# Partition sums in the second modulation: products with a column of ones instead of transposes and a VectorE sum

## The chip, the cores and the metric

The kernel runs on one core of a Trainium2 chip. The metric is the device time of one execution in microseconds; several executions are timed and the median is taken. One execution is recorded by the hardware profiler. The engines are TensorE (PE, with its weight loads listed apart as PEld), VectorE (DVE), ScalarE (ACT), GpSimd (POOL) and SyncE (SP).

## The reference

One layer of a hybrid backbone for 256 latent tokens and 256 context tokens of width 2048, all in float32. What matters here is the conditioning. A vector `c` of 2048 elements gives six modulation vectors of 2048 elements each:

```python
def adaln(cond, w_mod, b_mod):
    m = (jax.nn.silu(cond) @ w_mod + b_mod).reshape(cond.shape[:-1] + (6, D_MODEL))
    return tuple(jnp.expand_dims(m[..., i, :], -2) for i in range(6))

sh1, sc1, gt1, sh2, sc2, gt2 = adaln(c, w_mod[l], b_mod[l])
hx = modulate(rms_norm(x, g_mix[l]), sh1, sc1)
# ... four token mixers on hx @ w_in, gates, sum, output projection ...
x_mixed = x + gt1 * merge_branches(...)
hx2 = modulate(rms_norm(x_mixed, g_ffn[l]), sh2, sc2)
x = x_mixed + gt2 * swiglu(hx2, w_ffn_gate[l], w_ffn_up[l], w_ffn_down[l])
```

`sh1` and `sc1` are needed at once and are made at the start of the kernel. `gt1`, `sh2`, `sc2` and `gt2` are needed much later; making them is the "second modulation".

## The kernel before

**Weights as pieces.** All large weight matrices come in pieces of 128 x 1024 float32 (512 KB) through a ring of four slots. SP loads a piece into `RAW`. ACT rounds it to `HI` (L438), DVE subtracts to get `LO` (L771), and PE multiplies: each exact float32 product is made of three products of rounded operands, the three lines L1344 to L1346 and L1372 to L1374. Semaphore `lo_done` releases PE and also SP's next load; `used`, given by PE, lets ACT overwrite the slot.

**Stages.** First modulation and input products with it (to about 150 us), input projections with attention, pooling and LRU steps between the pieces (to about 440 us), a mixing loop `pe.Fori(1, 4)` whose first pass is unrolled ahead of it (to about 820 us), the output projection (to about 907 us), then the gated feed-forward part. Every engine has its order written out by hand: DVE and PE run through the same piece numbers `w`, and small steps are called after given pieces.

**Second modulation.** A group `g` is 512 columns of `w_mod`. POOL loads it in 16 row tiles of 128 x 512 (L408). DVE multiplies each tile by its 128 elements of silu(c), one per partition, and adds it to an accumulator (`mod_tile`, L871 and L873), so that after 16 tiles the 512 wanted numbers are the sums of the accumulator's columns over its 128 partitions. Groups 0 to 11 (`gt1`, `sh2`, `sc2`) are finished by two helpers; the last four (`gt2`) take another way and are not touched.

- `mod_turn(g, acc, bank)` on PE (L1490 to L1495) waits until the 16 tiles are in, transposes the four 128 x 128 blocks of the accumulator into one bank of PSUM (`turn`, L1340: the block is the loaded weight, the identity is streamed), and signals `mod_turned`.
- `mod_columns(g, bank)` on DVE (L876 to L882) waits for that, sums the 128 x 4 x 128 numbers over the innermost axis (L880), waits for its own result, adds the bias (L882) and signals `mod_read`. The results are four columns of `MC2`.

**Where they stand.** Group 0: PE after piece 44, DVE after piece 47 of the input projections (about 290 us). Groups 1 to 9: three per pass of the mixing loop, on PE after pieces 2, 17 and 28 (`MOD_TURN_AT`), on DVE after 6, 21 and 32 (`MOD_READ_AT`). Groups 10 and 11: in the output projection, on PE after pieces 12 and 27, on DVE after 17 and 31. `a2()` (L1112) needs group 11, and the feed-forward part's first step needs `a2`.

**Other small products that the prediction uses.** `mod1_turn` (L1439) multiplies a 128 x 128 float32 block, as weight, by 4 streamed columns (`PICK`); it belongs to the first modulation. `h2_turn` (L1725) multiplies 128 x 128 float32 blocks of tokens by a diagonal matrix of 128 columns. `mod_unit` (L1426) streams 256 columns against weights of 32 columns. L930 and L931 are the mask and the row maximum of the attention scores.

`Own` counts a DVE semaphore for waits of the engine on its own results; `own.enter` and `own.leave` only do arithmetic on that count for a loop.

Of the kernel before, what the change touches and what calls it, by code (L numbers as in the profile page):

```python
# [25 lines left out]
ALU = mybir.AluOpType  # L26
ACT = mybir.ActivationFunctionType
AX_X = mybir.AxisListType.X

P = 128  # L30
# [100 lines left out]
def build(nc, x, c, ctx, c_ctx, w_mod, b_mod, g_mix, g_ffn, g_final, w_in, w_pool, pool_scale,  # L131
# [3 lines left out]
    with ctxs:  # L135
        def sb(name, shape, dt=F32):
            return ctxs.enter_context(nc.sbuf_tensor(name, shape, dt))

        def sem(name):
            return ctxs.enter_context(nc.semaphore(name))  # L140
# [13 lines left out]
        PA = sb("PA", [P, P])  # L154
# [3 lines left out]
        MC2 = sb("MC2", [P, 4 * KT])  # L158
        A2 = sb("A2", [P, KT])
        EPSC = sb("EPSC", [P, 1])  # L160
        ST = sb("ST", [P, 64])
# [61 lines left out]
        ps = ctxs.enter_context(nc.psum_tensor("ps", [P, 8, BW], F32))  # L223
# [30 lines left out]
        def s(name):  # L254
            if name not in S:
                S[name] = sem(name)
            return S[name]
# [507 lines left out]
        def _(dve):  # L765
            own = Own(dve, own_v)
            tt, ts, stt = dve.tensor_tensor, dve.tensor_scalar, dve.scalar_tensor_tensor

            def low(p, j):
                dve.wait_ge(hi_done, p + 1)  # L770
                tt(LO[:, j % RING, :], RAW[:, j % RING, :], HI[:, j % RING, :], ALU.subtract).then_inc(lo_done, 1)  # L771
# [7 lines left out]
            dve.memset(ST[:, 48:49], 0.0).then_inc(lo_done, 1)  # L779
            dve.memset(ST[:, 49:50], 0.0).then_inc(lo_done, 1)  # L780
            dve.memset(RP, 0.0).then_inc(s("rp_zero"), 1)
            own.did(dve.memset(SCP, 0.0))
            own.did(dve.memset(SHP, 0.0)); own.wait()
            dve.wait_ge(s("cst_in"), 16)
# [76 lines left out]
            def mod_tile(g, k, acc):  # L861

                if isinstance(g, int) and g < EARLY:
                    src = MR[:, k % 2, :]
                    dve.wait_ge(s(f"mod_landed{k % 2}"), g * (KT // 2 * 16) + 16 * (k // 2 + 1))
                else:
                    src = MR4[:, k % 4, :]
                    dve.wait_ge(s(f"mod4_landed{k % 4}"), g * (KT // 4 * 16) + 16 * (k // 4 + 1 - EARLY * KT // 4))
                if k:
                    dve.wait_ge(s("mod_used"), g * KT + (k + 2))  # L870
                    i = stt(acc, src, SCF[:, 0, k:k + 1], acc, ALU.mult, ALU.add)  # L871
                else:
                    i = ts(acc, src, SCF[:, 0, k:k + 1], None, ALU.mult)  # L873
                i.then_inc(s("mod_used"), 1)

            def mod_columns(g, bank):  # L876

                dve.wait_ge(s("mod_turned"), g + 1)
                sums = MC2[:, bass.ds(g * 4, 4)]
                own.did(dve.reduce_sum(sums, ps[:, bank, :].rearrange("p (k n) -> p k n", k=4), AX_X))  # L880
                own.wait()
                tt(sums, sums, PA[:, bass.ds(g * 4 + 32, 4)], ALU.add).then_inc(s("mod_read"), 1)  # L882

            def straight(w):
                if w == 18:
# [16 lines left out]
                if w == 47:  # L902
                    mod_columns(0, 0)
# [154 lines left out]
            def merge(f, n, b):  # L1058

                dve.wait_ge(used, f * BLK + (MIX0 + 34 + 2 * n + 4))  # L1060
                dve.wait_ge(s("gate_read"), f * 4 + (n + 1))
                m = flat(MG[:, 3, :])
                if n == 0:
                    if not isinstance(f, int):
                        dve.wait_ge(s("mg_turned"), f)
                    tt(m, pair(b), flat(S4[:, n, :]), ALU.mult).then_inc(s("merge_read"), 1)
                    dve.wait_ge(s("merge_read"), f * 4 + (n + 1))
                    dve.memset(ST[:, 54:55], 0.0).then_inc(s("merge_add"), 1)
                else:
                    tt(flat(S4[:, n, :]), pair(b), flat(S4[:, n, :]), ALU.mult).then_inc(s("merge_read"), 1)  # L1070
                    dve.wait_ge(s("merge_read"), f * 4 + (n + 1))
                    dve.wait_ge(s("merge_add"), f * 4 + n)
                    tt(m, m, flat(S4[:, n, :]), ALU.add).then_inc(s("merge_add"), 1)
# [11 lines left out]
            dve.memset(ONES, 1.0).then_inc(s("branches_made"), 1)  # L1085

            with dve.Fori(1, 4) as f:
                own.enter(f, 1, 3)
                for w in range(BLK):
                    low(f * BLK + (MIX0 + w), w % 4)  # L1090
                    for t in MOD_AT[w]:
                        mod_tile(f * 3 + (t // KT - 1), t % KT, ACCB[:, t // KT, :])
                    if w in MOD_READ_AT:
                        mod_columns(f * 3 + (MOD_READ_AT.index(w) - 2), 4)
                    if w == 1:
                        merge(f - 1, 2, 0)
                    if w == 3:
                        merge(f - 1, 3, 2)
                    if w == 37:
                        merge(f, 0, 0)  # L1100
                    if w == 39:
                        merge(f, 1, 2)
                own.leave(1, 3)

            def merged_low(f):
                src = pair(6).rearrange("p b e -> p (b e)") if f == 3 else MG[:, f, :]
# [23 lines left out]
            for n in range(4):  # L1130
                for j in range(8):
                    low(OUT0 + 8 * n + j, j)
                    if n == 0 and j < 2:
                        merge(3, 2 + j, 2 * j)
                        merged_low(1 + j)
                    if n == 0 and j == 5:
                        merged_low(3)
                    if 8 * n + j == 4:
                        gate1_spread()
                    if 8 * n + j == 17:  # L1140
                        mod_columns(10, 6)
                    if 8 <= 8 * n + j < 24:
                        mod_tile(11, 8 * n + j - 8, ACCB[:, 0, :])
                    if 8 * n + j == 31:
                        mod_columns(11, 6)
                    if n and j == 3:
                        residual(n - 1)
                    if n == 2 and j >= 4:
                        dve.memset(ACC[:, j - 4, :], 0.0).then_inc(s("down_read"), 1)
# [185 lines left out]
        def _(pe):  # L1335
            mm = pe.matmul

            def turn(o, src, start=True):
                n = src.shape[0]
                return mm(o, src, IDENT[0:n, 0:n], start=start, stop=True, is_transpose=True, skip_group_check=True)  # L1340
# [149 lines left out]
            def mod_turn(g, acc, bank):  # L1490

                pe.wait_ge(s("mod_used"), g * KT + (KT + 2))
                for k in range(4):
                    i = turn(ps[:, bank, k * P:(k + 1) * P], acc[:, k * P:(k + 1) * P], start=k == 0)
                i.then_inc(s("mod_turned"), 1)  # L1495

            def straight(w):
                if w == 44:

                    pe.wait_ge(s("win_read"), 3)  # L1500
                    mod_turn(0, ACCM[:, 0, :], 0)
# [93 lines left out]
            for n, sl in enumerate(WIN_ORDER):  # L1595
# [11 lines left out]
                for j in range(2 if sl == S_VAL else 0, 8):  # L1607
                    p = WIN0 + 8 * n + j
# [16 lines left out]
            def tokens_of(src):  # L1625

                return lambda k, q: (src[:, k, 0, q * P:q * P + P], src[:, k, 1, q * P:q * P + P])
# [40 lines left out]
            with pe.Fori(1, 4) as f:  # L1668
                base = MIX0 + f * BLK
                for n in range(NB):  # L1670
# [4 lines left out]
                    for w in gate_group(base, n):  # L1675
# [3 lines left out]
                        if w in MOD_TURN_AT:  # L1679

                            i = MOD_TURN_AT.index(w) - 1
# [18 lines left out]
            def row_pass(p, j, lhs, q, o, k0, first, last):  # L1700

                ready(p)
                for t in range(2):
                    wh, wl = HI[:, j % RING, t * BW:(t + 1) * BW], LO[:, j % RING, t * BW:(t + 1) * BW]
                    xh, xl = lhs(k0 + t, q)
                    i = rows3(o, xh, xl, wh, wl, first and t == 0, last and t == 1)
                if q:
                    i.then_inc(used, 1)
                return i
# [40 lines left out]
            for q in range(2):  # L1750
                for j in (6, 7):
                    i = row_pass(OUT0 + 24 + j, j, tokens_of(HX), q, ps[:, 2 + q, :], 2 * j, False, j == 7)
# [59 lines left out]
            for half in range(2):  # L1812
                for n in (2 * half, 2 * half + 1):
                    i = mm(ps[:, 4 + n, :], ONES, ACCG[:, n, :], start=True, stop=True)
# [74 lines left out]
```

## Time and profile before

| | us |
|---|---|
| median of 3 runs | 1663.89 |
| lowest, highest | 1661.49, 1664.94 |
| the profiled execution, its own time | 1660.5 |
| span in its trace | 1658.6 |
| PE busy | 1618.6 (98%) |
| DVE busy | 1099.6 (66%) |
| ACT busy | 727.3 (44%) |
| chain that ended last: on PE | 89% |

The span runs from the first to the last recorded instruction. PE's busy time counts overlapping records of a pipelined engine, so 98% does not mean that PE works at its peak; how far apart instructions of one kind start tells more than their length. Idle time of DVE or ACT costs nothing where PE is not waiting for them.

### The profile page before, as it was taken

The page shows a single profiled execution, that of the slowest core. Times are in us where ns is not written, and L with a number is a line of the kernel's source. Part 1 is how long each engine was busy: PE and PEld are TensorE (multiplying, and loading weights), DVE is VectorE, ACT ScalarE, POOL GpSimd, SP SyncE. Part 2 cuts the span into 40 slices and gives each one's busy share as a digit, 9 for nine tenths or more (in the row PEclk, how much of TensorE's full clock was granted, in tenths as well). Part 3 has the DMA queues.
Part 4 walks back from the last instruction along what each step waited for, and adds up shares of the span by engine and source line. Part 5 has one row for each costly group of instructions (what it writes and reads, how often), then busy time and mean ns, then how long its engine had stood idle before and what let it go on. Part 6 is the DMA issues. An engine that isn't in the chain of part 4 may idle for free.

```text
span 1658.6 us, 22943 instructions
## 1 busy us (share of the span) xinstructions
PE 1618.6 (98%) x7915; PEld 1325.0 (80%) x7915; DVE 1099.6 (66%) x1253; ACT 727.3 (44%) x805; POOL 158.7 (10%) x294
## 2 busy tenths in 40 slices
PE   5999999999999999999999999999999999999998
PEld 3667888987788888888877788888888888888876
DVE  4233545878788888878977667767765556456577
ACT  5332233557744444444445544443444444434334
POOL 1002001000012212123010001101100000000000
PEclk8999999999999999999999999999999999999999
DMA  9997747554479979899676568778776566666653
GB/s 339 357 355 207 219 129 242 170 173 154 140 265 327 325 265 327 278 323 345 244 253 204 155 220 266 255 234 284 236 269 194 189 191 190 190 190 190 190 165 139
DMA packets 200248, 389.12 MB, mean 235 GB/s; under 512 B 14368, under 2 KB 47376, under 8 KB 199296
## 3 DMA queue, kind: packets, MB, share of 16 engines
q1 hardware_dynamic: 177168, 312.63, 58.7%
q0 software_dynamic: 23024, 75.74, 13.4%
q8 instruction: 36, 0.59, 0.1%
q14 instruction: 20, 0.16, 0.0%
HBM read 385.30 MB, written 3.01 MB: 234 GB/s over the span
## 4 chain that ended last, share of the span: by engine, by line
PE 89%; DVE 5%; ACT 3%; DMA 1%; issue 1%; SPq 0%; DVEq 0%; ACTq 0%
PE ps L1372 24%; PE ps L1374 23%; PE ps L1373 23%; PE ps L1344 5%; PE ps L1346 4%; PE ps L1345 4%; PE ps L1426 2%; DVE LO L771 2%; PE ps L1340 2%; DMA BR<-in_w_mod 1%; ACT HI L438 1%; PE ps L1533 0%; PE ps L1520 0%; DVE ATT L1017 0%; ACT ATT L609 0%
## 5 line engine op out<-in xcount | busy, mean ns | idle before, releaser
L771 DVE TENSOR_TENSOR LO<-RAW,HI 128x1024 fp32r<-128x1024 f32 x520 | 634.0, 1223 | 425.0 <-ACT HI L438 423.3
L438 ACT ACTIVATE HI<-RAW 128x1024 fp32r<-128x1024 f32 x520 | 548.6, 1060 | 765.6 <-PE ps L1374 657.3
L1372 PE MATMUL ps<-HI,H 128*128 128x512 f32 x1856 | 728.5, 393 | 3.7 <-DVE LO L771 3.1
L1374 PE MATMUL ps<-HI,H 128*128 128x512 f32 x1856 | 722.7, 389 | 0.0
L1373 PE MATMUL ps<-LO,H 128*128 128x512 f32 x1856 | 722.3, 389 | 0.0
L1372 PEld LDWEIGHTS ps<-HI,H 128*128 128x128 f32 x1856 | 348.4, 188 | 79.9 <-DVE LO L771 4.1
L1373 PEld LDWEIGHTS ps<-LO,H 128*128 128x128 f32 x1856 | 348.5, 188 | 72.8 <-issue 1.7
L1374 PEld LDWEIGHTS ps<-HI,H 128*128 128x128 f32 x1856 | 348.3, 188 | 72.9
L408 POOL DMA_DIRECT2D BR<-in_w_mod x224 | 120.4, 538 | 770.2 <-DVE BR L871 315.3
L871 DVE SCALAR_TENSOR_TENSOR BR<-BR,SCF 128x512 f32<-128x512 f32 (+1 forms) x210 | 156.9, 747 | 9.7 <-DMA BR<-in_w_mod 8.4
L1344 PE MATMUL ps<-H,HI 128*128 128x256 f32 (+1 forms) x384 | 127.7, 333 | 3.1 <-DVE LO L771 3.0
L1346 PE MATMUL ps<-H,LO 128*128 128x256 f32 (+1 forms) x384 | 123.7, 322 | 0.0
L1345 PE MATMUL ps<-H,HI 128*128 128x256 f32 (+1 forms) x384 | 123.6, 322 | 0.0
L1344 PEld LDWEIGHTS ps<-H,HI 128*128 128x128 f32 x384 | 73.7, 192 | 19.3 <-issue 13.8
L1346 PEld LDWEIGHTS ps<-H,LO 128*128 128x128 f32 x384 | 73.7, 192 | 5.6
L1345 PEld LDWEIGHTS ps<-H,HI 128*128 128x128 f32 x384 | 73.9, 192 | 5.2 <-issue 0.2
L1231 DVE TENSOR_TENSOR ATT<-ps,ATT 128x1024 f32<-128x1024 f32 x36 | 43.8, 1218 | 0.0
L1426 PE MATMUL ps<-BR 128*32 128x256 f32 x400 | 30.1, 415 | 8.2 <-DMA BR<-in_w_mod 8.2
L803 DVE TENSOR_TENSOR MC<-ps,PA 128x4 f32<-128x4 f32 x16 | 1.8, 156 | 53.8 <-PE ps L1439 53.8
L1340 PE MATMUL ps<-CST,BR 128*128 128x128 f32 (+1 forms) x145 | 22.2, 303 | 11.1 <-DVE BR L835 7.1
L1340 PEld LDWEIGHTS ps<-CST,BR 128*128 128x128 f32 (+1 forms) x145 | 19.4, 158 | 14.5 <-issue 9.1
L408 POOL DMA_DIRECT2D MR<-in_w_mod x32 | 17.5, 548 | 132.5 <-DVE ACCM L871 111.9
(252 smaller groups left out, 778.3 us busy)
## 6 DMA issues: line engine op xcount, KB each, us to landing
RAW<-in_w_gate SPq DMA_DIRECT2D x128, 512.0 KB, 4.8
BR<-in_w_mod POOLq DMA_DIRECT2D x224, 256.0 KB, 4.6
RAW<-in_w_ffn_gate SPq DMA_DIRECT2D x88, 512.0 KB, 3.7
RAW<-in_w_ffn_up SPq DMA_DIRECT2D x88, 512.0 KB, 3.8
RAW<-in_w_ffn_down SPq DMA_DIRECT2D x88, 512.0 KB, 3.6
RAW<-in_w_in SPq DMA_DIRECT2D x64, 512.0 KB, 4.7
BR<-in_w_mod SPq DMA_DIRECT2D x50, 512.0 KB, 9.1
RAW<-in_w_branch SPq DMA_DIRECT2D x32, 512.0 KB, 5.3
```

The lines of the kernel that those rows point to most:

```text
L408: pool.dma_start(slots[:, k % ring, :], w_mod[0, k * P:(k + 1) * P, bass.ds(2 * D + g * BW, BW)])\
L438: act.activation(HI[:, j % RING, :], RAW[:, j % RING, :], ACT.Copy).then_inc(hi_done, 1)
L771: tt(LO[:, j % RING, :], RAW[:, j % RING, :], HI[:, j % RING, :], ALU.subtract).then_inc(lo_done, 1)
L871: i = stt(acc, src, SCF[:, 0, k:k + 1], acc, ALU.mult, ALU.add)
L1340: return mm(o, src, IDENT[0:n, 0:n], start=start, stop=True, is_transpose=True, skip_group_check=True)
L1344: mm(o, wh, xh, start=first, stop=False, skip_group_check=True)
L1345: mm(o, wh, xl, start=False, stop=False, skip_group_check=True)
L1346: return mm(o, wl, xh, start=False, stop=last, skip_group_check=True)
L1372: mm(o, xh, wh, start=first and t == 0, stop=False, skip_group_check=True)
L1373: mm(o, xh, wl, start=False, stop=False, skip_group_check=True)
L1374: i = mm(o, xl, wh, start=False, stop=last and t == 1, skip_group_check=True)
L1426: m = mm(ps[32 * g:32 * g + 32, 6, 0:CW], silu[:, 4 * i + g, :], mod_raw(p + part)[:, g * CW:(g + 1) * CW], start=i + part == 0, stop=i == ...
```

## The change

The four transposes of a group become four plain float32 products of the same blocks with a column of ones, and each writes one column of PSUM: the sum over partitions is made on PE. DVE's sum over columns and the wait for it go away; the bias is added straight from PSUM. The column of ones, `ST[:, 59:60]`, is set once at the start. Since DVE's own wait has gone from the loop, the two calls that count it there go as well.

```diff
@@ -779,6 +779,7 @@
             dve.memset(RP, 0.0).then_inc(s("rp_zero"), 1)
+            own.did(dve.memset(ST[:, 59:60], 1.0))
             own.did(dve.memset(SCP, 0.0))
@@ -876,10 +877,7 @@
             def mod_columns(g, bank):
 
                 dve.wait_ge(s("mod_turned"), g + 1)
-                sums = MC2[:, bass.ds(g * 4, 4)]
-                own.did(dve.reduce_sum(sums, ps[:, bank, :].rearrange("p (k n) -> p k n", k=4), AX_X))
-                own.wait()
-                tt(sums, sums, PA[:, bass.ds(g * 4 + 32, 4)], ALU.add).then_inc(s("mod_read"), 1)
+                tt(MC2[:, bass.ds(g * 4, 4)], ps[:, bank, 0:4], PA[:, bass.ds(g * 4 + 32, 4)], ALU.add).then_inc(s("mod_read"), 1)
@@ -1085,7 +1083,6 @@
             with dve.Fori(1, 4) as f:
-                own.enter(f, 1, 3)
                 for w in range(BLK):
@@ -1100,7 +1097,6 @@
                     if w == 39:
                         merge(f, 1, 2)
-                own.leave(1, 3)
@@ -1491,7 +1487,7 @@
                 pe.wait_ge(s("mod_used"), g * KT + (KT + 2))
                 for k in range(4):
-                    i = turn(ps[:, bank, k * P:(k + 1) * P], acc[:, k * P:(k + 1) * P], start=k == 0)
+                    i = mm(ps[:, bank, k:k + 1], acc[:, k * P:(k + 1) * P], ST[:, 59:60], start=True, stop=True, skip_group_check=True)
                 i.then_inc(s("mod_turned"), 1)
```

## Rows read from the trace of the kernel before

**Rows 1.** The page: busy us, share of the span and instructions of each engine.
```profile
PE 1618.6 (98%) x7915; PEld 1325.0 (80%) x7915; DVE 1099.6 (66%) x1253; ACT 727.3 (44%) x805; POOL 158.7 (10%) x294
```

**Rows 2.** Stretches: length; busy PE, PEld, DVE, ACT, POOL; clock; DMA.
```profile
286.00:300.00 14.00, 13.86 (x68) 11.15 (x67) 8.47 (x15) 7.18 (x13) 1.08 (x2) 1.00 0.32 100
...
480.00:820.00 340.00, 340.00 (x1529) 281.35 (x1527) 279.84 (x313) 145.96 (x140) 78.51 (x146) 1.00 0.88 306
838.00:903.00 65.00, 65.00 (x292) 53.62 (x291) 48.82 (x52) 31.04 (x38) 7.52 (x14) 1.00 0.73 241
```

**Rows 3.** Groups of instructions from 480 to 820 us: busy, mean ns, idle before.
```profile
L1372 PE MATMUL ps<-HI,H 128*128 128x512 f32 x489 | 191.5, 392 | 0.0
...
L771 DVE TENSOR_TENSOR LO<-RAW,HI 128x1024 fp32r<-128x1024 f32 x121 | 148.1, 1224 | 43.5 <-ACT HI L438 42.6
```

**Rows 4.** Timeline of PE about a group's four transposes: start, length, instruction.
```profile
488.81 0.39 PE L1374 MATMUL ps<-HI,H 128*128 128x512 f32 x1
489.04 0.60 PE L1340 MATMUL ps<-CST,BR 128*128 128x128 f32 x4
489.39 0.48 PE L1372 MATMUL ps<-HI,H 128*128 128x512 f32 x1
489.71 0.40 PE L1373 MATMUL ps<-LO,H 128*128 128x512 f32 x1
```

**Rows 5.** Timeline about a `mod1_turn` (4 streamed columns), PE and weight loads.
```profile
148.07 0.28 PE L1346 MATMUL ps<-H,LO 128*128 128x256 f32 x1
148.08 0.53 PEld L1439 LDWEIGHTS ps<-BR 128*128 128x128 f32 x4
...
148.76 0.28 PE L1345 MATMUL ps<-H,HI 128*128 128x256 f32 x1
...
148.88 0.28 PE L1346 MATMUL ps<-H,LO 128*128 128x256 f32 x1
```

**Rows 6.** Timeline of PE about an `h2_turn` of eight products of 128 columns.
```profile
922.17 0.40 PE L1346 MATMUL ps<-HI,H 128*128 128x512 f32 x1
922.41 1.95 PE L1725 MATMUL ps<-ATT,BR 128*128 128x128 f32 x16
...
924.43 0.39 PE L1345 MATMUL ps<-LO,H 128*128 128x512 f32 x1
```

**Rows 7.** Timeline about a `mod_unit`: 16 weights of 32 columns.
```profile
144.97 1.07 PE L1426 MATMUL ps<-BR 128*32 128x256 f32 x16
```

**Rows 8.** Views of L880 (with its waits: us, times) and L1439: ns min/median/max, starts.
```profile
L880 DVE TENSOR_REDUCE MC<-ps x12: 681/684/691, 290.0 to 898.4; 128x512 f32 x9, 128x4 f32<-128x512 f32 x3
...
  PE ps L1340: 3.6, 1
...
L1439 PE MATMUL ps<-BR x32: 167/252/273, 32.8 to 148.4; 128*128 128x4 f32 x32
```

**Rows 9.** Timeline of PE and DVE about group 0, and PE's next late start.
```profile
289.33 0.60 PE L1340 MATMUL ps<-CST,ACCM 128*128 128x128 f32 x4
...
289.97 0.69 DVE L880 TENSOR_REDUCE MC<-ps 128x4 f32<-128x512 f32 x1 [3.57 <-PE ps L1340]
290.69 0.16 DVE L882 TENSOR_TENSOR MC<-MC,PA 128x4 f32<-128x4 f32 x1
290.77 0.42 DVE L930 TENSOR_TENSOR ps<-ps,ATT 128x256 f32<-128x256 f32 x1
...
296.91 1.23 DVE L771 TENSOR_TENSOR LO<-RAW,HI 128x1024 fp32r<-128x1024 f32 x1 [1.79 <-ACT HI L438]
...
297.75 0.39 PE L1374 MATMUL ps<-HI,H 128*128 128x512 f32 x1
...
298.48 0.28 PE L1345 MATMUL ps<-H,HI 128*128 128x256 f32 x1
```

**Rows 10.** Timelines: PE's late start at the loop's end; DVE after group 11.
```profile
820.24 0.47 PE L1372 MATMUL ps<-HI,H 128*128 128x512 f32 x1 [0.18 <-DVE LO L771]
...
900.54 1.23 DVE L771 TENSOR_TENSOR LO<-RAW,HI 128x1024 fp32r<-128x1024 f32 x1 [1.02 <-ACT HI L438]
```

## The prediction, made before the changed kernel was run

> **What bounds the kernel now.** I read the page's busy times first [rows 1]: PE is at 98% of the span, DVE at 66%. Since PE's busy share counts overlapping records, it proves little alone. The stretch table [rows 2] shows the two stretches in which eleven of the twelve groups lie, 480 to 820 us and 838 to 903 us: PE is busy for all of them, at the full clock (1.00, that is 2.4 GHz). The groups of the first stretch [rows 3] settle it: 489 first products of a piece's triples stood idle before them for 0.0 us, though those are the instructions that would wait for `LO`; DVE's `LO` instead waited 42.6 us in total for ACT. So in these stretches PE's own stream of instructions sets the time, DVE has slack, and whatever PE has to issue more or less is paid or gained one for one. The timeline [rows 4] gives the stream's beat: products of 512 columns start 0.23 us apart (488.81 to what follows at 489.04), although each record is 0.39 us long. I therefore price PE work by how far it pushes the next starts apart, never by record lengths.
>
> **Removed from PE: four transposes per group.** In [rows 4] the last 512-column product before the block starts at 488.81 and the second one after it at 489.71, 0.90 us. Without the block that would be two beats, 0.45 us. (The second one is taken because the first one's record, 0.48 us instead of 0.39, begins 0.09 us early.) So four transposes cost 0.45 us, 0.11 each. The other ten in these stretches look the same: 0.35 or 0.36 us from the block's start to the next record.
>
> **Added to PE: four plain float32 products per group, each with a full 128-column weight and one streamed column.** The trace has no product of one column. It has two near rows. `mod1_turn` issues two products of 4 columns and leaves four records of load and matmul [rows 5], and `h2_turn` eight products of 128 columns and leaves sixteen [rows 6], where the four transposes left four [rows 4]. So a plain float32 product is two load-and-matmul pairs and a transpose is one: the change puts eight pairs in the place of four. What does a pair cost?
> - 4 columns [rows 5]: from 148.07 to 148.76 is 0.69 us for four pairs and two beats; the beat of the 256-column products there is about 0.12 us (148.76, 148.88), so 0.69 - 0.24 = 0.45 us, 0.113 per pair. The weight loads show why: four in 0.53 us, each started 0.11 us after the other.
> - 128 columns [rows 6]: 924.43 - 922.17 - 0.45 = 1.81 us for sixteen pairs, 0.113 per pair.
>
> 4 and 128 columns cost the same, so the loads set the pace and not what is streamed; one column is nearly 4, and I take 0.113. Eight pairs are 0.90 us. A load of a whole block can't run under a product of one column, while the 512-column products around hide theirs. The net is 0.90 - 0.45 = +0.45 us per group.
>
> From below, the cheapest pair in the trace has a weight of 32 columns only: sixteen matmuls in 1.07 us [rows 7], (1.07 - 0.28)/15 = 0.053 us apart (0.28 being the length of a 256-column record, [rows 5]). At that price eight pairs are 0.42 us and the change is free on PE. From above, I know no row dearer than 0.12, the beat of 256-column products; eight would be 0.96 us, net +0.51.
>
> The Trainium skill has a rule that speaks against the change: its page "TensorE: Matmul & The Clock Gate", section "Terms", says that transpose mode is four times faster for FP32. By it four plain products would cost 4 x 0.45 = 1.8 us, the net would be +1.35 us per group and about +15 us in all; rows 4 and 6 show two to one, and I go by the rows.
>
> **Removed from DVE.** Twelve sums of 0.684 us [rows 8] and the wait for each, 0.72 us from one start to the next at group 0 (289.97 to 290.69, [rows 9]); the addition of 0.16 us stays, now reading PSUM. About 12 x 0.72 = 8.6 us of DVE time goes. In the mixing loop and the output projection no instruction of PE waits for it [rows 3], so it is worth nothing there. One place could use it: at the end of the loop PE waits for `LO` once, 0.18 us [rows 10]. But the last sum of the loop stands after piece 32 of 40, and a DVE that waits for ACT 42.6 us over 121 pieces [rows 3], 0.35 us at each, has lost the 0.72 us gained after a few of the eight left; I count nothing. For group 11 the sum starts at 898.4 [rows 8], and behind it DVE stands idle for ACT 1.02 us before 900.54 [rows 10]: nothing either.
>
> **Group 0 is different** [rows 9]. DVE had waited 3.57 us for the transposes when it starts the sum at 289.97, and behind the sum stand the attention's mask and maximum, ACT's exponentials and then `LO` at 296.91, for which PE starts late: from 297.75 to 298.48 is 0.73 us where the beats (0.23 + 0.12) ask 0.35, so PE loses 0.38 us. With the change the last pair starts at 289.33 + 7 x 0.113 = 290.12 and ends, with a length of 0.17 to 0.25 us [rows 8], at about 290.33. Add 0.04 us for DVE to be released (289.93 to 289.97 before) and 0.08 from the addition's start to the next (290.69 to 290.77): L930 starts at about 290.45, 0.3 us earlier than before. So `LO` is ready 0.3 us sooner while PE arrives 0.45 us later: the 0.38 us wait is gone and 0.45 - 0.38 = 0.07 us is paid.
>
> **Waits and the rest.** `mod_turned` comes 0.45 us later. L880 has waited for the transposes once in twelve times, 3.6 us, and that is group 0 [rows 8, 9]; at the others DVE comes at least four pieces later in the order and finds them done, with piece on piece of 2.7 us (twelve beats) between, so 0.45 us more is not felt. Nobody new waits. The loads of `w_mod` on POOL hang on `mod_used`, which DVE's tiles give as before, and SP's loads on `lo_done`; both queues are passed by nothing. The column of ones is one more small write among DVE's first ones, before it waits for the first constants to land: free; if that cover were gone it would cost under 0.1 us. Dropping the loop's count removes no instruction.
>
> **Sum.** 11 x 0.45 + 0.07 = +5.0 us. The profiled execution, 1660.5 us, would become 1665.5. It lies 3.4 us under the median of 1663.89, so the median would become 1668.9, 0.30% more. I take 0.2%, 3.3 us, as what a measurement of this kernel can tell from no change.
>
> **Rivals.**
> 1. *A pair with one column is cheap.* If a pair's price did follow what is streamed, or if the second load of the same block were quick, pairs would come at the 0.053 us of [rows 7]: eight for 0.42 us, net zero on PE and 0.3 us or so won at group 0. Time 1663.6: not slower. It decides from 0.095 us a pair downward (8 x 0.095 - 0.45 = 0.31, times 11 is 3.4 us). Against it stands that 4 and 128 columns cost the same [rows 5, 6], and that all those weights are of 128 columns like the new ones. Chance 0.12. The Trainium skill, page "TensorE: Matmul & The Clock Gate", section "Back-to-back issue gap", goes further and gives a floor of about 25 ns for 1 to 64 columns; by that, called an estimate, eight pairs would be 0.2 us and the kernel about 3 us faster, but 0.113 us for 4 columns in rows 5 contradicts it.
> 2. *DVE's relief pays.* If PE's stream were after all held by DVE in the loop, 0.72 us less per group would give 9 x 0.72 = 6.5 us against 5.0, about 1662.4. It needs PE waiting for `LO` in the loop; [rows 3] has 0.0 us. Chance 0.04.
> 3. *A product of one column leaves more than two pairs, or pairs of 0.2 us.* At sixteen pairs a group costs 1.81 us [rows 6], net +1.36, and the time is 1663.9 + 11 x 1.36 = 1679. Rows 5 and 6 both show two. Chance 0.04.
> 4. *The clock.* In a block of one-column products the array has little to do; if the clock fell to its lower level (1.2 GHz), each 512-column beat behind it would about double. The block with 4 columns in [rows 5] is followed by the beat of before it (148.76, 148.88), and in [rows 2] the clock is 1.00 in the stretch with group 0's transposes. Were the clock low for 2 us behind each of twelve blocks, it would cost some 12 us: 1681. Chance 0.02.
>
> **How the numbers follow.** The forecast has 0.76. Its own range takes pairs from 0.107 (the 0.53 us of four loads less a load's 0.19, over three, is 0.113; [rows 6] gives (1.95 - 0.28)/15 = 0.111) to 0.12, so +4.5 to +5.7 us, and the scatter of the runs shown (2.4 under to 1.1 over their median): 1666.0 to 1671.5. The whole range reaches down over rivals 1 and 2 to 1662 and up to 1672, and leaves out rivals 3 and 4 and the tails, under 2 in 10. Slower by over 0.2%: nine tenths of the forecast's 0.76, with rivals 3 and 4, and some rest, 0.74. Within 0.2%: the other tenth, most of rivals 1 and 2, 0.21. Faster: 0.05.
>
> **What would show it.** In the changed kernel's timeline about 489 us: eight records of L1491 in the place of four, and 1.35 us instead of 0.90 between the last 512-column product before and the second after; if it is 0.9, rival 1 holds. The loop's pass should be 1.35 us longer. No reduction left in `mod_columns`, and DVE's busy time down by 8 us. PE's late start at 298 us gone. `LO` before the products idle as before (0.0); were it more than that, DVE is a bound and rival 2 is alive. A clock below 1.00 between 290 and 900 us would speak for rival 4. The prediction fails first if the price per pair, read off 4 and 128 columns, does not hold at one.

## The result, and the profile after

| | before | changed |
|---|---|---|
| median | 1662.11 us (20 runs) | 1665.24 us (20 runs) |
| lowest, highest | 1660.51, 1664.94 | 1664.21, 1669.03 |
| profiled execution, own time | 1660.5 | 1665.21 |
| span in the trace | 1658.6 | 1663.5 |

The ratio is 1.0021, with a 95% interval of 1.0015 to 1.0027: the changed kernel is slower, by 2.5 to 4.5 us. The forecast had been slower by 5.0 us, 1668.9 us, in a range from 1662 to 1672.

The page of the changed kernel, busy times as in [rows 1]:

```profile
PE 1622.5 (98%) x7963; PEld 1330.5 (80%) x7963; DVE 1091.3 (66%) x1242; ACT 727.5 (44%) x805; POOL 158.6 (10%) x294
```

PE has 48 more matmul records, four for each of the twelve groups, and DVE has lost 8.3 us. The groups of the stretch in which the mixing loop lies now (484 to 824 us), as in [rows 3]:

```profile
L1368 PE MATMUL ps<-HI,H 128*128 128x512 f32 x484 | 189.3, 391 | 0.0
...
L771 DVE TENSOR_TENSOR LO<-RAW,HI 128x1024 fp32r<-128x1024 f32 x119 | 145.6, 1223 | 54.1 <-ACT HI L438 53.1
```

(L1368 is what L1372 was.) PE is idle for 0.0 us ahead of these products, as before, and DVE waits for ACT 53.1 us instead of 42.6: the nine sums that it was relieved of there, 6.5 us, have become waiting (the rest of the 10.5 us is in part that this stretch holds two of its `LO` fewer, 2.4 us). The timeline at group 1's block, as in [rows 4], PE and weight loads:

```profile
489.03 0.40 PE L1370 MATMUL ps<-HI,H 128*128 128x512 f32 x1
489.26 0.95 PE L1490 MATMUL ps<-ST,BR 128*128 128x1 f32 x8
490.08 0.48 PE L1368 MATMUL ps<-HI,H 128*128 128x512 f32 x1
490.39 0.40 PE L1369 MATMUL ps<-LO,H 128*128 128x512 f32 x1
...
489.03 1.09 PEld L1490 LDWEIGHTS ps<-ST,BR 128*128 128x128 f32 x8
```

Eight matmuls and eight loads stand where four were, and from the last 512-column product before to the second after it is 490.39 - 489.03 = 1.36 us, where it was 0.90. Eight loads in 1.09 us, the last 0.19 long, start 0.90/7 = 0.129 us apart on average, which fits a first gap of 0.23 (the first load is made under the 512-column product ahead, and the next one waits for that product's beat to end) and six of 0.11.

Group 0 and PE's start that had been late, as in [rows 9]; the column of ones is read at L1490, the addition is L880, the attention's mask L928:

```profile
289.16 0.95 PE L1490 MATMUL ps<-ST,ACCM 128*128 128x1 f32 x8
...
290.15 0.16 DVE L880 TENSOR_TENSOR MC<-ps,PA 128x4 f32<-128x4 f32 x1 [3.89 <-PE ps L1490]
290.23 0.42 DVE L928 TENSOR_TENSOR ps<-ps,ATT 128x256 f32<-128x256 f32 x1
...
298.01 0.39 PE L1370 MATMUL ps<-HI,H 128*128 128x512 f32 x1
298.24 0.28 PE L1340 MATMUL ps<-H,HI 128*128 128x256 f32 x1
298.35 0.28 PE L1341 MATMUL ps<-H,HI 128*128 128x256 f32 x1
```

From the block's start to the mask it is 1.07 us (1.44 before), and PE goes from its 512-column products to those of 256 columns without a gap. From 289.16 to 298.35 it is 9.19 us; before, 289.33 to 298.48, it was 9.15. Group 0 costs 0.04 us net.

**Stage by stage.** Three profiles of either kernel, each of another execution, cut at PE's own landmarks: the second block of attention scores (L1520 of before), the second block of products with the values (L1533), the first products of the last LRU group (L1558), the spread of gate 1 (L1697), the last `h2_turn` (L1725). Differences of starts in their timelines, in us:

| stretch | before, three profiles | changed, three profiles |
|---|---|---|
| first instruction to scores | 283.16, 282.77, 282.89 | 282.99, 282.98, 282.12 |
| scores to values (group 0 in it) | 39.97, 40.51, 40.07 | 40.36, 40.13, 40.02 |
| values to LRU | 107.15, 107.15, 107.15 | 107.15, 107.17, 107.15 |
| LRU to gate 1 (groups 1 to 9) | 404.59, 404.58, 404.53 | 408.38, 408.41, 409.30 |
| gate 1 to last `h2_turn` (10, 11) | 92.41, 92.42, 92.45 | 93.31, 93.27, 93.28 |
| from there to the end | 731.3, 731.3, 731.4 | 731.3, 731.3, 731.3 |

The rows behind the fourth and fifth lines of this table, of before and then of the changed kernel (the view of the second one ends inside the row of L1693, so it counts three of its eight products; only starts are used):

```profile
430.28 1.02 PE L1558 MATMUL ps<-BR 128*128 128x512 f32 x2
...
834.87 3.60 PE L1697 MATMUL ps<-BR 128*128 128x512 f32 x8
...
927.28 1.95 PE L1725 MATMUL ps<-ATT,BR 128*128 128x128 f32 x16
```

```profile
430.50 1.02 PE L1554 MATMUL ps<-BR 128*128 128x512 f32 x2
...
838.88 1.45 PE L1693 MATMUL ps<-BR 128*128 128x512 f32 x3
...
932.19 1.95 PE L1721 MATMUL ps<-ATT,BR 128*128 128x128 f32 x16
```

So 3.8 us come in with groups 1 to 9, 0.42 each, and 0.87 us with groups 10 and 11: 4.7 us in every profile. PE does wait in these two stretches, but alike in both kernels: 2.0 us and twice some 0.3 us ahead of group 1's block, 0.18 us once between the blocks of groups 9 and 10, and 0.6 to 1.1 us three times behind group 11. From group 1's block to gate 1 alone it is 346.03 to 346.06 us before and 349.84 to 349.88 in the changed kernel. The value 409.30 has 0.9 us of another origin, which lies ahead of group 1's block (below). All of the rest is equal or scatters for both kernels.

### The profile page after: what moved, and what is told of

Same layout as the page of the kernel before. It is cut to its first block, busy times and chain, and to the rows that moved or that the text cites. A ratio compares the mean times of both kernels' runs of the same rounds, so it can differ in the third digit from the quotient of the medians.

```text
span 1663.5 us, 23013 instructions
## 1 busy us (share of the span) xinstructions
PE 1622.5 (98%) x7963; PEld 1330.5 (80%) x7963; DVE 1091.3 (66%) x1242; ACT 727.5 (44%) x805; POOL 158.6 (10%) x294
## 4 chain that ended last, share of the span: by engine, by line
PE 87%; DVE 5%; ACT 3%; DMA 2%; issue 1%; SPq 1%; DVEq 0%; POOLq 0%; ACTq 0%
PE ps L1368 23%; PE ps L1369 23%; PE ps L1370 23%; PE ps L1340 4%; PE ps L1341 4%; PE ps L1342 4%; PE ps L1422 2%; DVE LO L771 2%; DMA MR<-in_w_mod 2%; PE ps L1336 1%; ACT HI L438 1%; DMA BR<-in_w_mod 1%; PE ps L1490 1%; SPq L281 1%; PE ps L1529 0%
## 5 line engine op out<-in xcount | busy, mean ns | idle before, releaser
L1368 PE MATMUL ps<-HI,H 128*128 128x512 f32 x1856 | 728.3, 392 | 3.7 <-DVE LO L771 3.0
L1370 PE MATMUL ps<-HI,H 128*128 128x512 f32 x1856 | 722.6, 389 | 0.0
L1368 PEld LDWEIGHTS ps<-HI,H 128*128 128x128 f32 x1856 | 348.5, 188 | 80.0 <-DVE LO L771 4.1
L1422 PEld LDWEIGHTS ps<-BR 128*32 128x32 f32 x400 | 11.4, 114 | 20.4 <-issue 15.7
L1340 PE MATMUL ps<-HI,H 128*128 128x512 f32 x64 | 25.9, 405 | 1.7 <-DVE H L860 1.7
```

What stands on the lines that cost most here:

```text
L1340: mm(o, wh, xh, start=first, stop=False, skip_group_check=True)
L1368: mm(o, xh, wh, start=first and t == 0, stop=False, skip_group_check=True)
L1370: i = mm(o, xl, wh, start=False, stop=last and t == 1, skip_group_check=True)
L1422: m = mm(ps[32 * g:32 * g + 32, 6, 0:CW], silu[:, 4 * i + g, :], mod_raw(p + part)[:, g * CW:(g + 1) * CW], start=i + part == 0, stop=i == ...
```

## The experiments

The times of the kernel before that were taken beside each set of kernels are those in the ratios. All executions pooled, the kernel before has 121, with a mean of 1661.97 us and a median of 1661.55; differences of means below are against these, with a 95% interval that allows for the small number of executions of some kernels.

**PE's half alone.** DVE keeps its sum.

```diff
-                    i = turn(ps[:, bank, k * P:(k + 1) * P], acc[:, k * P:(k + 1) * P], start=k == 0)
+                    i = mm(ps[:, bank, k:k + 1], acc[:, k * P:(k + 1) * P], ST[:, 59:60], start=True, stop=True, skip_group_check=True)
...
                 own.did(dve.reduce_sum(sums, ps[:, bank, :].rearrange("p (k n) -> p k n", k=4), AX_X))
                 own.wait()
-                tt(sums, sums, PA[:, bass.ds(g * 4 + 32, 4)], ALU.add).then_inc(s("mod_read"), 1)
+                tt(sums, ps[:, bank, 0:4], PA[:, bass.ds(g * 4 + 32, 4)], ALU.add).then_inc(s("mod_read"), 1)
```

> The products with ones on PE as in the changed kernel, and DVE's sum over 512 columns kept (its result is overwritten by the bias addition, which reads the products). Theory A (each group's block is eight load-and-matmul pairs instead of four, and nothing else counts): the block takes 1.36 us between the last 512-column product before and the second after, every group pays 0.43 us, and since DVE is not relieved PE's late start at 298 us stays and group 0 pays too: 12 x 0.43 = +5.2 us over the kernel before. Theory B (the changed kernel's median is only 3.1 us up because DVE, relieved of its sums, gives about 1.7 us back somewhere): this kernel gets nothing back, so it is 1.7 us or more above the changed kernel, and the kernel without the sums alone (e2) is 1.7 us faster than before. Under A it is 0.4 us above the changed kernel.

Measured: 1667.3 us (5 runs), ratio 1.0035 (1.0021 to 1.0049), +5.5 us (3.3 to 7.7) in the mean. Its profile has 4.7 us more from LRU to gate 1 and 0.85 more to the last `h2_turn`, of which 0.9 in the first are no part of the change (below), and 41.49 us from scores to values, 0.98 to 1.5 more than before. Of that, group 0's block and the kept delay are 0.34 us, at 298 us; most of the rest is a second late start of PE near 321 us, which comes and goes in all kernels (at the end of this section). Theory A's 5.2 is met, in an interval that is wide. Its distance from the changed kernel, 1.7 us of the means, is uncertain by 2.2, so it does not tell A's 0.4 from B's 1.7.

**DVE's half alone.**

```diff
-                sums = MC2[:, bass.ds(g * 4, 4)]
-                own.did(dve.reduce_sum(sums, ps[:, bank, :].rearrange("p (k n) -> p k n", k=4), AX_X))
-                own.wait()
-                tt(sums, sums, PA[:, bass.ds(g * 4 + 32, 4)], ALU.add).then_inc(s("mod_read"), 1)
+                tt(MC2[:, bass.ds(g * 4, 4)], ps[:, bank, 0:4], PA[:, bass.ds(g * 4 + 32, 4)], ALU.add).then_inc(s("mod_read"), 1)
```

> PE transposes as before; DVE leaves out the sum over the 128 columns of each block and adds the bias to four columns of the transposed block (this part of the computation is left out, so gt1, sh2 and sc2 are not the reference's). Theory A: only group 0 gains; L930 starts some 0.7 us earlier and PE's late start near 298 us of 0.38 us goes: -0.4 us in all, not measurable. Theory B (DVE's relief gives time back): -1.7 us or more, and PE's idle time before the first product of a triple is lower in the loop.

Measured: 1660.71 us (11 runs), ratio 0.9996 (0.9987 to 1.0005), -0.8 us (-1.7 to 0.1) in the mean, between theory A's -0.4 and theory B's -1.7. The profile shows where there is nothing to win: from group 1's block to gate 1 it has 346.02 us, as before, and from gate 1 to the last `h2_turn` 92.40. Rival 2 of the prediction, that DVE's relief pays in the loop, is out. At group 0 PE's late start at 298 us is gone, as theory A has it; but scores to values is 40.52 us, no shorter than before, since PE is late by 0.68 us at 320 us instead (at the end of this section).

**Plain products with the identity, 128 columns.** DVE as before.

```diff
-                    i = turn(ps[:, bank, k * P:(k + 1) * P], acc[:, k * P:(k + 1) * P], start=k == 0)
+                    i = mm(ps[:, bank, k * P:(k + 1) * P], acc[:, k * P:(k + 1) * P], IDENT, start=k == 0, stop=True, skip_group_check=True)
```

> The kernel before with its four transposes per group made as plain float32 products with the identity, 128 columns each; the outcome is the same transposed block and DVE is as before. Theory A (pairs set the price, columns do not): eight pairs per group, 1.36 us between the last 512-column product before and the second after, as with one column, and +5.2 us over the kernel before, the same as e1. Rival C (what is streamed has a part in the price): the block is longer than 1.36 us, and at double the columns' cost (0.107 us for 128 at two cycles each, added to the load) up to 2.2 us and +15 us.

Measured: 1666.64 us (7 runs), ratio 1.0029 (1.0018 to 1.004), +4.8 us (4.1 to 5.4). The timeline at group 1's block:

```profile
489.20 0.40 PE L1374 MATMUL ps<-HI,H 128*128 128x512 f32 x1
489.43 1.06 PE L1494 MATMUL ps<-CST,BR 128*128 128x128 f32 x8
490.24 0.48 PE L1372 MATMUL ps<-HI,H 128*128 128x512 f32 x1
490.56 0.39 PE L1373 MATMUL ps<-LO,H 128*128 128x512 f32 x1
```

490.56 - 489.20 = 1.36 us with 128 streamed columns, as with one. What is streamed has no part in the price up to 128 columns, and leaving the transpose mode costs the same 0.46 us whatever the products are used for. Rival C is out. Four products take 1.36 - 0.45 = 0.91 us and the four transposes of the same blocks took 0.45: twice as much. The Trainium skill's four to one ("TensorE: Matmul & The Clock Gate", "Terms") is not what this stream shows.

This kernel has blocks as long as the changed kernel's and DVE's sums as before, and its mean lies 0.9 us (0.2 to 1.7) above the changed kernel's: that is what the relief of DVE is worth by these executions, with the 0.4 us of the late start inside the interval.

**Each product twice.**

```diff
+                    for _ in range(2):
-                    i = mm(ps[:, bank, k:k + 1], acc[:, k * P:(k + 1) * P], ST[:, 59:60], start=True, stop=True, skip_group_check=True)
+                        i = mm(ps[:, bank, k:k + 1], acc[:, k * P:(k + 1) * P], ST[:, 59:60], start=True, stop=True, skip_group_check=True)
```

> The changed kernel with each product with ones issued twice into the same column. Theory A: sixteen pairs per group, block 0.90 us longer (2.26 us instead of 1.36), 12 x 0.90 = 10.8 us over the changed kernel and about 15.5 over the kernel before. If part of a group's price is given back elsewhere in proportion (theory B's form on PE: some of the PE stream has hidden slack), the step is smaller, at the measured ratio 3.1/4.8 about 7 us. Rival D (the clock): with 1.8 us of one-column products in a row the granted clock would fall below 1.00 behind a block, and 512-column products would start 0.43 us apart there.

Measured: 1677.11 us (4 runs), ratio 1.0095 (1.008 to 1.0111), +15.5 us (13.9 to 17.1). The timeline at group 1's block, and the row of the stretch behind it, as in [rows 2] (the clock is the number ahead of the last two):

```profile
491.31 0.40 PE L1370 MATMUL ps<-HI,H 128*128 128x512 f32 x1
491.54 1.84 PE L1491 MATMUL ps<-ST,BR 128*128 128x1 f32 x16
493.25 0.48 PE L1368 MATMUL ps<-HI,H 128*128 128x512 f32 x1
493.57 0.40 PE L1369 MATMUL ps<-LO,H 128*128 128x512 f32 x1
```

```profile
494.00:498.00 4.00, 4.00 (x19) 3.30 (x18) 2.18 (x5) 1.06 (x1) 1.08 (x2) 1.00 0.96 337
```

The block is 493.57 - 491.31 = 2.26 us, 0.90 more, and the kernel is 11.7 us (give or take 1.6) above the changed one (15.5 - 3.85), where theory A had 10.8. Its profile is closer: from group 1's block to gate 1 it has 357.88 us, 8.0 more than the changed kernel, 0.89 for each of nine groups. PE's stream has no slack, and the clock stays at its upper level (1.00) even behind 1.8 us of one-column products: rival 4 of the prediction and rival D are out.

**The two kernels again.** No edit; three runs of this sort.

> The changed kernel, unchanged, once more. Its first profile is 4.9 us longer than that of the kernel before, of which 4.7 us are in the stretch after 489 us where PE is never late; its median was only 3.1 us up. Theory A (the 4.7 us are the change's price in every execution, and the 1.6 us between it and the medians are chance in the DMA-paced stretches before 489 us): from the first block of the mixing loop to the end 4.7 us more than before, to 0.1 us, and a median 4 to 5 us above. Theory B (relief of DVE is worth 1 to 2 us, in stretches before 489 us): the same 4.7 us behind 489 us, but the median again near 3 us above, and the first block of the loop earlier than in the kernel before run beside it.

> The kernel before once more, for its trace and for the scatter. Its first profile was among its shortest executions (1660.5 us against a median of 1662.1). Theory A: a time within 0.1% of the kernel before, 1660.2 to 1665 us; from the first block of the mixing loop (489.04 us in the first trace) to the end of the span the trace shows 1169.6 us again, to 0.1 us; what differs lies before it, in stretches where loads are waited for, and there in steps of up to 1 us.

> The changed kernel once more, to pool with its 30 executions (mean 3.7 us above the kernel before, where the traces' sum is 4.7). Traces: 368.8 us from the loop's entry to the product that spreads gate 1, 93.3 to the last h2 block, as in the two profiles so far, 3.8 and 0.9 us more than before. If the 1 us between mean and sum is chance, the pooled mean rises over 4; if it is a relief of DVE at group 0 worth more than 0.4 us, it stays at 3.5 to 4 and e9 and e10 come out as theory B says.

> The kernel before once more, for a third trace and the scatter: 364.98 us from the loop's entry to the product that spreads gate 1 and 92.4 to the last h2 block as in both profiles so far. From group 0's block to the second set of attention products 33.8 to 34.9 us. Where a stretch of lower clock lies behind PE's wait of 2 us at 453 us, 0.9 us more between there and the mixing loop, as in e1 to e4; this would show the scatter of both kernels (4 us) to be the clock's, not the change's.

Measured: the changed kernel 1665.66 us (10 runs), ratio 1.0025 (1.0015 to 1.0034), and 1665.55 us (10 runs), 1.0025 (1.0015 to 1.0034); the kernel before 1661.2 us (11 runs), 0.9995 (0.9985 to 1.0004), and 1661.33 us (11 runs), 1.0001 (0.9992 to 1.001). Pooled, 40 executions of the changed kernel have a mean of 1665.81 us: +3.85 us (3.4 to 4.3). The traces are those of the table above: theory A's 4.7 us, to 0.1, in all three profiles of either kernel once the 0.9 us are set aside. The times fall between the theories: the two medians are 4.0 and 4.2 us above those of the kernel before beside them, at theory A's lower end (4 to 5) and over theory B's 3, while the pooled mean stays in the 3.5 to 4 us that the third expectation gave to a relief of DVE.

The 0.9 us are seen in the third profile of the changed kernel. Before the mixing loop PE waits 1.94 to 1.99 us for a `LO` that stands behind LRU steps on DVE, in every profile of every kernel. Its timeline behind that wait, and then that of the first profile:

```profile
451.84 0.50 PE L1368 MATMUL ps<-HI,H 128*128 128x512 f32 x1 [1.98 <-DVE LO L771]
...
453.65 0.63 PE L1368 MATMUL ps<-HI,H 128*128 128x512 f32 x1
454.08 0.63 PE L1369 MATMUL ps<-LO,H 128*128 128x512 f32 x1
...
456.52 0.40 PE L1369 MATMUL ps<-LO,H 128*128 128x512 f32 x1
456.75 0.40 PE L1370 MATMUL ps<-HI,H 128*128 128x512 f32 x1
```

```profile
453.03 0.50 PE L1368 MATMUL ps<-HI,H 128*128 128x512 f32 x1 [1.98 <-DVE LO L771]
...
454.98 0.39 PE L1370 MATMUL ps<-HI,H 128*128 128x512 f32 x1
455.21 0.39 PE L1368 MATMUL ps<-HI,H 128*128 128x512 f32 x1
```

In the one, products start 0.43 us apart from about 453.2 to 456.2, which is the lower level, 1.2 GHz, and in the other 0.23 us apart: the same wait of 2 us is followed by a stretch of low clock in some executions and in others not. It was in six of fourteen profiles here (this one, the four of the first set of experiments and the one with the late group 0), for 0.9 us each from the wait to group 1's block. Three of the six have no product with ones at all (those without sums, with the identity and with the late group 0). So this is no sign of rival 4, though the prediction named a clock below 1.00 between 290 and 900 us as one. The like lies behind two earlier waits: behind one of 2.43 us at 87 us in six profiles, and behind one of 2.98 us at 154 us in ten. This is a part of the scatter, in both kernels: executions of the kernel before with a mean clock of 0.993 or more took 1661.4 us in the mean (74 of 101 for which the clock is known), those below 1663.3 (27).

**Group 0 as before, the rest changed.**

```diff
+                if isinstance(g, int) and g == 0:
+                    sums = MC2[:, bass.ds(g * 4, 4)]
+                    own.did(dve.reduce_sum(sums, ps[:, bank, :].rearrange("p (k n) -> p k n", k=4), AX_X))
+                    own.wait()
+                    tt(sums, sums, PA[:, bass.ds(g * 4 + 32, 4)], ALU.add).then_inc(s("mod_read"), 1)
+                    return
...
+                    if isinstance(g, int) and g == 0:
+                        i = turn(ps[:, bank, k * P:(k + 1) * P], acc[:, k * P:(k + 1) * P], start=k == 0)
+                        continue
```

> The changed kernel, with group 0 alone done as before (four transposes, DVE's sum). Theory A: PE saves 0.43 us in group 0's block and gets back its late start of 0.38 us at 298 us, so the time is that of the changed kernel, within 0.1 us of the sum; behind 489 us nothing changes against it. Theory B (what the changed kernel's median is better than the sum comes from DVE being earlier at group 0, ahead of a stretch in which loads are waited for): 1 to 2 us slower than the changed kernel.

Measured: 1666.44 us (9 runs), ratio 1.0026 (1.0016 to 1.0036), +4.35 us (3.6 to 5.1). That is 0.5 us above the changed kernel's pooled mean, with an uncertainty of 0.8: between theory A's nothing and theory B's 1 to 2, nearer to A. Its profile has 408.39 and 93.32 us in the two stretches, as the changed kernel, and 40.41 from scores to values, within what both kernels show there.

**Group 0's read moved behind the attention's mask and maximum**, in the kernel before; run twice.

```diff
-                if w == 47:
-                    mod_columns(0, 0)
...
+                    if w == w0 + 4 and half:
+                        mod_columns(0, 0)
                     if w == w0 + 6:
```

> The kernel before, with DVE's read of group 0 (sum and bias) moved behind the attention's four mask-and-maximum steps of the same piece. Theory A: L930 does not wait for the transposes any more and starts at once when the scores are there, 1 us or more earlier; PE's late start of 0.38 us at 298 us goes; 0.4 us faster than before in the trace between group 0's block and the next 256-column products, nothing behind 489 us, not measurable in the median. Theory B (DVE being earlier ahead of the stretch in which loads are waited for is worth more than PE's late start): 1 to 2 us faster than the kernel before.

> The kernel e5 once more (DVE's read of group 0 behind the attention's mask and maximum). Theory A: 33.41 us from group 0's block to the second set of attention products, as in e5's trace, or up to 0.6 us more where tiles of w_mod land late; 0.4 us faster than before in the sum, and the pooled median of both runs no more than 0.8 us below the kernel before. Theory B: again 1 to 1.7 us below it.

Measured: 1660.15 us (11 runs), ratio 0.999 (0.9981 to 0.9999), and 1659.69 us (11 runs), 0.9991 (0.9982 to 1.0); pooled -1.7 us (-2.3 to -1.1). DVE's timeline in the second of them:

```profile
284.53 0.74 DVE L871 SCALAR_TENSOR_TENSOR ACCM<-MR,SCF,ACCM 128x512 f32<-128x512 f32 x1
285.19 0.42 DVE L928 TENSOR_TENSOR ps<-ps,ATT 128x256 f32<-128x256 f32 x1
...
289.45 0.68 DVE L880 TENSOR_REDUCE MC<-ps 128x4 f32<-128x512 f32 x1
290.16 0.16 DVE L882 TENSOR_TENSOR MC<-MC,PA 128x4 f32<-128x4 f32 x1
```

The mask begins as soon as DVE is free, with no wait for the transposes [rows 9: 3.57 us], and the sum is done behind. From scores to values the two profiles have 39.58 and 39.59 us, against 39.97 to 40.51 in the kernel before: 0.4 to 0.9 us less. Behind it both profiles are as before; ahead of it the first of them has 2.1 to 2.5 us more, with a low clock behind both early waits. So the traces are theory A's and the times are not: the pooled median is 1.6 us below the kernel before, where theory A allowed 0.8 and theory B had 1 to 1.7. This is the only kernel here that beats both.

**Group 0's sum three times.**

```diff
+                if isinstance(g, int) and g == 0:
+                    for _ in range(2):
+                        own.did(dve.reduce_sum(sums, ps[:, bank, :].rearrange("p (k n) -> p k n", k=4), AX_X))
+                        own.wait()
```

> The kernel before, with DVE's sum of group 0 made three times in a row (same result). It doubles and trebles the delay that the change takes away at group 0. Theory A (a DVE that is later at group 0 holds PE just by that much, through the late start at 298 us): two more sums of 0.72 us put L930 1.44 us later, PE's late start grows from 0.38 to 1.8 us, and the kernel is 1.4 us slower, nothing more behind it. Theory B (the delay costs more than the late start, because the loads behind it come later too; e5 was 1.5 us faster where A gives 0.4): clearly more than 1.4 us, some 2.5 us or more. Rival E (slack hides part of it, as tiles waited for do not come earlier for an earlier DVE): under 1.4 us.

Measured: 1663.2 us (11 runs), ratio 1.001 (1.0001 to 1.0019), +1.5 us (0.4 to 2.6). Theory A's 1.4 is met, but theory B's 2.5 is still inside the interval, so the times alone do not decide. The timeline of PE does, as in [rows 9]:

```profile
298.07 0.39 PE L1378 MATMUL ps<-HI,H 128*128 128x512 f32 x1
...
300.05 0.35 PE L1348 MATMUL ps<-H,HI 128*128 128x256 f32 x1 [1.59 <-DVE LO L771]
300.24 0.28 PE L1349 MATMUL ps<-H,HI 128*128 128x256 f32 x1
```

From 298.07 to 300.24 it is 2.17 us, where the kernel before has 0.73 [rows 9]: 1.44 us more for two sums of 0.72. From scores to values it is 42.03 us, 1.5 to 2.1 more than before. A delay of DVE at group 0 costs its own length and, in this profile, no multiple of it.

**A second late start, at about 320 us.** What makes the second line of the table scatter is one place, some 31 us behind group 0's block, where PE may have to wait for `LO` again. The kernel without sums shows it, DVE and then PE:

```profile
314.97 0.75 DVE L871 SCALAR_TENSOR_TENSOR ACCM<-MR,SCF,ACCM 128x512 f32<-128x512 f32 x1 [1.10 <-DMA MR<-in_w_mod]
...
318.65 1.23 DVE L771 TENSOR_TENSOR LO<-RAW,HI 128x1024 fp32r<-128x1024 f32 x1
...
319.93 0.39 PE L1339 MATMUL ps<-H,HI 128*128 128x256 f32 x1 [0.68 <-DVE LO L771]
```

DVE waits for tiles of `w_mod` to land, works without a pause from there to `LO`, and PE is late. PE's starts were set back there by about 0.9 us in this profile and in that of PE's half alone, by 0.6 in one of three of the kernel before (the other two 0.1 or nothing), by 0.4 at most in the three of the changed kernel, and by nothing in the two with the read moved. An earlier DVE does not do away with it by itself, as the kernel without sums shows; whether it makes it rarer would take more profiles than there are here.

## Why the prediction was right, and where its size was off

**The bound.** That PE's stream sets the time in the stretches of eleven groups, at one for one, is shown: doubling the products added 11.7 us for a predicted 10.8 (8.0 us over groups 1 to 9 in its trace, 0.89 each), and taking DVE's sums away moved nothing there.

**The price of a pair.** 0.113 us, read off 4 and 128 columns [rows 5, 6], held at one column: the block is 1.36 us (predicted 1.35), eight records of 128-column loads. The forecast's one unknown was bounded from both sides and taken from the right row. The rival with cheap pairs (0.053 us) and the one with sixteen records are out. The floor of about 25 ns that the Trainium skill gives for small products ("TensorE: Matmul & The Clock Gate", "Back-to-back issue gap") is not reached here: with weights of 128 columns in float32 a pair is 0.113 us, whatever it streams.

**The step mis-sized by a little.** The prediction carried 0.45 us from each block to the end. The blocks cost 0.46, but the sum over groups 1 to 9 is 3.8 us, 0.42 each: within some ten products behind a block the two streams' starts draw nearer by 0.03 us and then stay. A pass of the loop is 1.27 us longer, where the prediction said 1.35. For eleven groups this makes 4.7 us instead of 5.0. Why the products behind the transposes were a little slower was not tried.

**Group 0.** Right, in each of its steps: the mask begins 0.37 us sooner after the block's start (0.3 predicted), PE's late start is gone, and the group costs 0.04 us (0.07 predicted).

**The absolute time.** The forecast was put on a median of three runs, 1663.89 us. With 121 executions the median of the kernel before is 1661.55. The three were drawn from a scatter of several us; 1.8 us (1663.89 - 1662.11) of the 3.7 between forecast and measurement are this alone. The profiled execution, 1660.5 us, plus 4.7 would have been 1665.2, and the profiled execution of the changed kernel took 1665.21, which is close by luck too: the stretches ahead of the loop scatter by 1 us from profile to profile. The prediction's own range for the forecast has a slip in its upper end: 1663.9 + 5.7 + 1.1 is 1670.7, not 1671.5. The measured 1665.24 us lies below the forecast's own range, from 1666.0 us up, and inside the wide one, which goes down to 1662 for the sake of rivals that did not come true: that it fell there is in part luck. With the 1.8 us added it would be 1667.0 and in both.

**What stays open.** Traces say 4.7 us, the pooled executions 3.85 (3.4 to 4.3). Two causes were looked at. DVE's relief at group 0 might be worth more than PE's late start: the kernel with the read moved says so (-1.7 us, where its traces have 0.4 to 0.9 less), the ones without any sums (-0.8) and with group 0 as before (+0.5 against the changed kernel) leave room for it, the one with the identity products, which keeps DVE's sums, lies 0.9 us (0.2 to 1.7) above the changed kernel, and the one with the sum three times speaks against it. The second late start is the place where such a gain could lie, but the profiles do not show that an earlier DVE does away with it. Or chance in the clock: a mean clock of 0.992 or less was recorded in 4 of 40 executions of the changed kernel and in 27 of 101 of the kernel before; among the others the means are 1665.57 and 1661.38, a difference of 4.2, which would be 0.3 of the missing 0.85 us. Whether the change makes the low stretches rarer, by moving PE's later waits against them, or whether 4 of 40 is luck, no run here settles.

## What to carry to other kernels

Where PE's stream is the bound, work taken off VectorE is worth only what some product waits for, and a replacement on PE is paid in full: here 8.3 us of VectorE bought 0.4 us in the traces, at group 0, and 5 us of PE were spent on it. Count a small float32 product by the records it leaves and the columns of its weight, not by the columns that it streams; one plain product of a 128 x 128 block cost as much as two transposes of it here. The wait that cost something, VectorE standing 3.6 us before transposes with the attention's steps behind it, was cured by moving two lines: 0.4 us in the traces and 1.7 us in the mean time, of which the difference is not explained.

## What the runs showed of the hardware

- A plain float32 product with a weight of 128 columns costs 0.226 to 0.228 us of a packed stream, in two load-and-matmul pairs, whether it streams 1, 4 or 128 columns; a float32 transpose of the same block costs 0.11, one pair.
- After a wait of 2 us on PE the clock fell to 1.2 GHz for some 3 us in six of fourteen profiles, at 0.9 us each, and not in the others, at the same wait in the same order of work; after waits of 2.4 and 3.0 us it fell in six and ten of the fourteen. Blocks of eight one-column products (sixteen pairs), 1.8 us, did not bring it down.
- Nine in ten executions of the kernel before lie within about 4 us (0.25%), all 121 within 7.5 us, and the recorded mean clock, in its third digit, goes along with a part of it (1.9 us between the means of the two classes).
